# Four seams of a two-layer decoder kernel: where rows are normalised, where one unit is multiplied, in which turn tiles go, and which banks the first units use

## The chip, the cores and the metric

The kernel runs on one NeuronCore of one Trainium2 chip. Its engines are named as in the profile: PE (TensorE) for matmuls, DVE (VectorE), ACT (ScalarE), POOL (GpSimd) and SP (SyncE, which issues the DMAs here). The metric is the device time of one execution in microseconds (us); lower is better.

## The reference, cut to what matters

Two layers over a sequence of 1024 rows of 1024 float32 values. Layer 0 has a gated delta-net mixer with 8 heads, layer 1 a forgetting attention with 16 heads. Both end in the same tail:

```
y = (mixer output) @ w_out                      # 1024x1024 @ 1024x1024
x = layer_norm(DN_ALPHA * x + y, ln_g[i], ln_b[i])
gate = sigmoid(x @ ple_w_gate[i])
x = x + gate * (p[i] @ ple_w_proj[i])
```

`layer_norm` takes mean and variance of each row, then multiplies by `g` and adds `b`.

## The kernel before

Every product of full precision is made of three matmuls (high by high, high by low, low by high), with the operands split by ACT (high part, a copy) and DVE or POOL (low part, a subtraction). Rows go in 8 tiles of 128, columns in halves of 512, the inner dimension in 8 blocks k of 128. So one half of one tile is 8 x 3 = 24 matmuls of 128x512, and a whole tile is 48.

The program is a row of stages, each a `Phase`: an own set of buffers and semaphores, and a barrier over all engines at its end. In order: input transpose; `delta_net` (gdn); `mixer_out` (m0); `gated_embedding` (e0); `fox_values` (fv); `fox_attention` (fa); `mixer_out` again (m1); `gated_embedding` again (e1). Within a stage each engine runs its instructions in the order in which they are written, and waits for semaphores of the others. A helper (`Step`) makes each DVE, ACT and POOL instruction finish before the next begins.

**gdn.** For each head, 64 steps `s` interleave the projection of the next head with the delta rule of the last one. In the last round (`it == H`) no head is left to project, and `part_work` puts parts of m0's product there: a part is one half of one tile over the inner blocks k = 0 to 6 (the heads that are done), 21 matmuls. There are `PARTS = 7` of them, the two halves of tiles 0, 1, 2 and the first half of tile 3. From step 15 on each step takes one k (three matmuls); what isn't done by step 59 (`AT_O_SUMS`) follows in a row at step 60. DVE adds each part to ALPHA times the residual in `take_part`, at the steps in `TAKE_PARTS`, into rows of `x1`. At step 62 (`AT_O_NORM`) DVE finishes the last head in two instructions (lines 915 and 916).

**m0 and m1** (`mixer_out`). `o_part(t)` splits tile t of the mixer's output (ACT `o_hi`, then DVE `o_lo`, line 1130). PE multiplies tile by tile into four PSUM tensors `out[t % 4]`. DVE then, for each tile: two mixes (residual plus product, lines 1158 or 1160) with a `bn_stats` each, `bn_aggr`, a wait for ACT's 1/sqrt (lines 1119 and 1120), the normalising instruction (1168) and the multiplication by the gain (1172). POOL adds the shift and writes the tile to `x1` (line 1182); for the last tile DVE does that itself (1173). DVE's `o_part(t + 2)` stands between `bn_aggr` and the normalising instruction. In m0 the tiles 0 to 2 are short (only k = 7 is left: 6 matmuls each, and one piece of `o_part`), tile 3 is half short, and 4 to 7 are whole. They run in the order 0 to 7. In m1 all tiles are whole; tiles 0 and 1 run together while `w_out` arrives. Both stages begin with nine rounds of small matmuls (`warm_up`).

**e0 and e1** (`gated_embedding`). PE transposes tiles of `x1` (`flip_piece`), ACT and DVE split them into `a_hi`, `a_lo` (two buffers), and PE multiplies them with the gate weights. These come through a ring of 4 half-row blocks that SP fills; block n waits until block n - 4 is split. In e0 the finished tiles are transposed again into `xh`, `xl` for layer 1.

**fa**. `project` makes the units of pair 0 (four units of 24 matmuls: q and k, two halves) before there are any scores. All units go to one PSUM bank, `unit`, and `take_unit` (ACT) copies each out before the next begins. After the four units of a pair come `cross` (POOL), `square` (ACT), `sum_squares` (PE), `root` (ACT) and the multiplication by the gains (DVE, line 2128), and then the first score.

Of the kernel before, what the change touches and what calls it, by code (L numbers as in the profile page):

```python
# [7 lines left out]
F32R = mybir.dt.float32r  # L8
# [241 lines left out]
PARTS = 7  # L250
TAKE_PARTS = (28, 30, 37, 44, 51, 58, 61)
# [736 lines left out]
def mixer_out(nc, c, ring, ahead, after, o, parts, residual, w_out, ln_g, ln_b, w_hi, w_lo, x1, name):  # L988


    with Phase(nc, name) as ph:
# [19 lines left out]
        alone = parts // 2  # L1011

        def pieces(t):

            return [slice(KT - 1, KT)] if t < alone else [slice(0, 4), slice(4, KT)]

        def pieces_before(t):
            return sum(len(pieces(n)) for n in range(t))
# [6 lines left out]
        def _(sp):  # L1025
            def load_x(t):
                if t >= alone + 2:
                    sp.wait_ge(mixed_made, t - 1)
                sp.dma_start(old[:, t % 2], residual[t * P:(t + 1) * P, :]).then_inc(x_loaded[t % 2], 16)
# [6 lines left out]
            load_x(alone)  # L1036
            load_x(alone + 1)
# [5 lines left out]
            for t in range(alone + 2, NT):  # L1043
                load_x(t)

        @block.tensor
        def _(pe):
            def multiply(t, k, halves=(0, 1)):
                if t >= 4:
                    pe.wait_ge(mixed_made, t - 3)  # L1050
                y = out[t % 4]
                for half in halves:
                    if k not in own_ks(t, half):
                        continue
                    first = k == own_ks(t, half)[0]
                    cols = slice(half * HALF, (half + 1) * HALF)
                    pe.matmul(y[:, cols], o_hi[:, t % OB, k, :], w_hi[:, k, cols], start=first, stop=False)  # L1057
                    pe.matmul(y[:, cols], o_hi[:, t % OB, k, :], w_lo[:, k, cols], start=False, stop=False)
                    mm = pe.matmul(y[:, cols], o_lo[:, t % OB, k, :], w_hi[:, k, cols], start=False,
                                   stop=(k == KT - 1))  # L1060
# [13 lines left out]
            for t in range(0 if parts else 2, NT):  # L1074
                pe.wait_ge(o_low, pieces_before(t + 1))
                if t == NT - 1:

                    for half in range(2):
                        for k in range(KT):
                            multiply(t, k, (half,))  # L1080
                    break
                for k in range(KT):
                    multiply(t, k)

        def halves(t):
            for n, ks in enumerate(pieces(t)):
                yield pieces_before(t) + n, ks, o[:, ks, t * P:(t + 1) * P]

        @block.scalar
        def _(act):  # L1090
# [23 lines left out]
            for t in range(NT):  # L1114
# [3 lines left out]
                r = rstd[:, t % 2:t % 2 + 1]  # L1118
                step(act.activation(r, moments[:, t % 2, 1:2], ACT.Ln, bias=eps[:, 0:1]))
# [3 lines left out]
        def _(dve):  # L1123
# [20 lines left out]
            for t in range(NT):  # L1144
                b = t % 2
                if t >= alone:
                    dve.wait_ge(x_loaded[b], 16 * ((t - alone) // 2 + 1))
                if t >= 2:

                    dve.wait_ge(x_made, t - 1)  # L1150
                for half in range(2):
                    cols = slice(half * HALF, (half + 1) * HALF)
                    if half == 0 and t == NT - 1:
                        dve.wait_ge(half_made, 1)
                    else:
                        dve.wait_ge(y_made, t + 1)
                    if 2 * t + half < parts:
                        mix = dve.tensor_tensor(mixed[:, b, cols], x1[:, t, cols], out[t % 4][:, cols], ALU.add)
                    else:
                        mix = dve.scalar_tensor_tensor(mixed[:, b, cols], old[:, b, cols], ALPHA, out[t % 4][:, cols],  # L1160
                                                       ALU.mult, ALU.add)
# [1063 lines left out]
```

## Time and profile before

| | us |
|---|---|
| median of 3 runs | 1812.75 |
| lowest and highest | 1812.61, 1815.48 |
| the profiled execution | 1813.67 |
| its span in the trace | 1811.9 |

The rows of the trace that are used stand in the section after the next. Times in them are microseconds from the start of the span. A timeline row is: start, duration, engine, line, operation, output<-inputs, count, and in brackets how long the engine was idle before it and what ended that. PE's matmuls overlap, so their duration (0.39) is longer than the distance from one to the next.

### The profile page before, as it was taken

Reading aid. Unit: us, or ns where it says so; the run is one execution under the profiler, and the core shown is the slowest. Engines: PE = TensorE matmul, PEld = TensorE weight load, DVE = VectorE, ACT = ScalarE, POOL = GpSimd, SP = SyncE. Lnnn points to the kernel's source line nnn. Section 1 sums busy time; section 2 is a strip of 40 time slices with the busy share of each in tenths; the row PEclk is TensorE's granted clock in tenths of the full one; section 3 lists DMA queues with packets and bytes.
Section 4 is the critical chain, followed back from the end, with each engine's and each line's share of the span. In section 5 each row is a group of like instructions: output and inputs, shape, how many; then the busy total and the mean of one; then the engine's idle time right before and its main releaser. Section 6 shows DMA issues by size and latency. Waiting matters only on the chain. (4 is left out here: it accounts for less than half of the span.)

```text
span 1811.9 us, 29013 instructions
## 1 busy us (share of the span) xinstructions
PE 1711.3 (94%) x11245; PEld 1304.0 (72%) x11245; DVE 909.1 (50%) x1712; ACT 756.8 (42%) x1248; POOL 299.1 (17%) x243
## 2 busy tenths in 40 slices
PE   7999999999999987979989999999999999898898
PEld 5777777777777765868877887666666665687687
DVE  3767576675767724654430300244444544565433
ACT  3446354463645542142231211465556565530411
POOL 2222132221321251200000000222212121012000
PEclk9999999999999998989989999999999999899899
DMA  5121110211101121131130200211111101040311
GB/s 131 48 60 34 26 48 12 48 36 36 42 19 36 59 94 59 35 125 44 41 118 1 70 25 23 56 33 42 48 31 43 42 21 42 15 163 34 117 44 50
DMA packets 113080, 92.86 MB, mean 51 GB/s; under 512 B 19697, under 2 KB 95665, under 8 KB 112945
## 3 DMA queue, kind: packets, MB, share of 16 engines
q1 hardware_dynamic: 112944, 91.02, 17.5%
q8 instruction: 90, 1.47, 0.3%
q14 instruction: 46, 0.37, 0.1%
HBM read 82.51 MB, written 8.49 MB: 50 GB/s over the span
## 5 line engine op out<-in xcount | busy, mean ns | idle before, releaser
L481 PE MATMUL gdn_unit<-part_hi,gdn_w_hi 128*128 128x512 f32 x512 | 232.2, 454 | 0.0
L483 PE MATMUL gdn_unit<-part_hi,gdn_w_lo 128*128 128x512 f32 x512 | 201.7, 394 | 0.0
L482 PE MATMUL gdn_unit<-part_lo,gdn_w_hi 128*128 128x512 f32 x512 | 200.8, 392 | 0.0
L2088 DVE CUSTOM_DVE_ANT_0 fa_probs<-fa_scores,fa_decay 128x896 f32<-128x896 f32 (+7 forms) x128 | 97.0, 757 | 121.6 <-PE fa_scores L1900 74.0
L875 DVE SCALAR_TENSOR_TENSOR x<-gdn_raw,gdn_taps,x 128x512 f32<-128x512 f32 x144 | 119.7, 832 | 5.1
L1852 PE MATMUL fa_unit<-part_hi,fa_w_hi 128*128 128x512 f32 x256 | 115.0, 449 | 4.8 <-ACT fa_qk L1999 3.4
L446 POOL TENSOR_TENSOR gdn_w_lo<-ring,gdn_w_hi 128x1024 fp32r<-128x1024 f32 x31 | 75.4, 2434 | 253.9 <-ACT gdn_w_hi L676 253.9
L483 PEld LDWEIGHTS gdn_unit<-part_hi,gdn_w_lo 128*128 128x128 f32 x512 | 96.2, 188 | 21.6
L2034 ACT ACTIVATE fa_probs_t<-fa_turned 128x512 f32<-128x512 f32 (+1 forms) x96 | 52.3, 544 | 139.3 <-PE fa_turned L1917 138.7
L481 PEld LDWEIGHTS gdn_unit<-part_hi,gdn_w_hi 128*128 128x128 f32 x512 | 97.0, 189 | 16.5 <-issue 3.6
L2028 ACT ACTIVATE fa_probs<-fa_probs,fa_top 128x896 f32<-128x896 f32 (+7 forms) x128 | 99.4, 777 | 22.5 <-DVE fa_top L2088 18.9
L482 PEld LDWEIGHTS gdn_unit<-part_lo,gdn_w_hi 128*128 128x128 f32 x512 | 97.3, 190 | 12.8 <-issue 3.6
L1289 PE MATMUL e_gate<-e_w_hi,e_a_hi 128*128 128x512 f32 x256 | 103.0, 402 | 2.8 <-DVE e_a_lo L1426 2.8
L1854 PE MATMUL fa_unit<-part_hi,fa_w_lo 128*128 128x512 f32 x256 | 100.7, 394 | 0.0
L1917 PE MATMUL fa_turned<-ident,fa_probs 128*128 128x128 f32 x576 | 96.6, 279 | 3.8 <-ACT fa_probs L2028 2.6
L1853 PE MATMUL fa_unit<-part_lo,fa_w_hi 128*128 128x512 f32 x256 | 100.1, 391 | 0.0
L1291 PE MATMUL e_gate<-e_w_hi,e_a_lo 128*128 128x512 f32 x256 | 100.1, 391 | 0.0
L1290 PE MATMUL e_gate<-e_w_lo,e_a_hi 128*128 128x512 f32 x256 | 99.8, 390 | 0.0
L1917 PEld LDWEIGHTS fa_turned<-ident,fa_probs 128*128 128x128 f32 x576 | 68.4, 140 | 41.2 <-issue 15.6
L1057 PE MATMUL m_y<-part_hi,m_o_hi 128*128 128x512 f32 x207 | 82.4, 398 | 7.9 <-DVE m_o_lo L1130 7.9
L2095 DVE COPY fa_probs_t<-fa_turned 128x512 f32<-128x512 f32 (+3 forms) x96 | 47.1, 491 | 75.8 <-PE fa_turned L1917 74.8
L1900 PE MATMUL fa_scores<-fa_qk 64*128 64x512 f32 (+3 forms) x384 | 79.3, 517 | 2.6 <-DVE fa_qk L2128 1.7
(307 smaller groups left out, 3644.4 us busy)
## 6 DMA issues: line engine op xcount, KB each, us to landing
ring<-in_gdn_w_in_dram SPq DMA_DIRECT2D x32, 512.0 KB, 4.1
ring<-in_ple_w_gate_dram SPq DMA_DIRECT2D x32, 256.0 KB, 3.0
ring<-in_fox_w_in_dram SPq DMA_DIRECT2D x32, 256.0 KB, 3.1
ring<-in_fox_w_in_dram SPq DMA_DIRECT2D x16, 512.0 KB, 4.7
fa_decay<-c_rows_scratch SPq DMA_DIRECT2D x64, 128.0 KB, 3.1
in_x_tile<-in_x_dram SPq DMA_DIRECT2D x8, 512.0 KB, 6.3
gdn_g_bc<-g_rows_scratch SPq DMA_DIRECT2D x8, 512.0 KB, 8.5
x_scratch<-x SPq DMA_DIRECT2D x8, 512.0 KB, 2.9
```

The costliest lines, as they stand in the source:

```text
L481: pe.matmul(out, w_hi[:, j % 2, k, :], xh[:, k, ts], start=(k == 0), stop=False)
L482: pe.matmul(out, w_hi[:, j % 2, k, :], xl[:, k, ts], start=False, stop=False)
L483: mm = pe.matmul(out, w_lo[:, j % 2, k, :], xh[:, k, ts], start=False, stop=(k == KT - 1))
L875: step(dve.scalar_tensor_tensor(out, shifted, weight, out, ALU.mult, ALU.add), conv_made if part == TAPS - 1 else None)
L1289: pe.matmul(out[:, cols], hi, w_hi[:, k, cols], start=first, stop=False)
L1290: pe.matmul(out[:, cols], hi, w_lo[:, k, cols], start=False, stop=False)
L1291: mm = pe.matmul(out[:, cols], lo, w_hi[:, k, cols], start=False, stop=end)
L1852: pe.matmul(out, w_hi[:, j % 2, k, :], xh[:, k, ts], start=(k == 0), stop=False)
L1853: pe.matmul(out, w_hi[:, j % 2, k, :], xl[:, k, ts], start=False, stop=False)
L1854: mm = pe.matmul(out, w_lo[:, j % 2, k, :], xh[:, k, ts], start=False, stop=(k == KT - 1))
L1917: mm = pe.transpose(turned[by][:, b * P:(b + 1) * P], probs[:, n % 3, j * P:(j + 1) * P], c["ident"][:])
L2028: step(act.activation(own, own, ACT.Exp, bias=top[:, n % 4:n % 4 + 1], scale=-1.0, accum_out=total[:, p % 2, e, head:head + 1]), exped)
```

## The change

Four things are done.

1. `PARTS` becomes 8: the second half of tile 3 is a part too. It runs at step 60 of the last round, after the seventh, and DVE takes it at step 61.
2. In `mixer_out` with parts (m0) the tiles go in the turns 0, 4, 1, 5, 2, 6, 3, 7, short and whole ones alternating. In both m0 and m1, DVE's `o_part(i + 2)` moves from behind `bn_aggr` to ahead of the mixes. In m0 the warm-up is 4 rounds, not 9.
3. The last tile's mixes go straight to its rows of `x1`, its mean, variance and 1/sqrt to a small tensor `final`, and `mixer_out` ends there. `gated_embedding` loads gain and shift again (two DMAs that write 512 KB each) and normalises the tile in two DVE instructions at t = 4; PE waits for that before it transposes tile 7. To make room, `a_hi`, `a_lo` lie in `part_hi`, `part_lo`.
4. In fa the units 0 to 3 go to the four banks of `scores`; `unit` is used from unit 4 on.

```diff
-PARTS = 7
-TAKE_PARTS = (28, 30, 37, 44, 51, 58, 61)
+PARTS = 8
+TAKE_PARTS = (28, 30, 37, 44, 51, 58, 60, 61)
...
+        turns = (0, 4, 1, 5, 2, 6, 3, 7) if parts else tuple(range(NT))
+        whole = [t for t in turns if 2 * t + 1 >= parts]
...
-            warm_up(pe, c, out[3])
+            warm_up(pe, c, out[3], 4 if parts else 9)
...
-                r = rstd[:, t % 2:t % 2 + 1]
-                step(act.activation(r, moments[:, t % 2, 1:2], ACT.Ln, bias=eps[:, 0:1]))
+                r, var = rstd[:, t % 2:t % 2 + 1], moments[:, t % 2, 1:2]
+                if t == NT - 1:
+                    r, var = final[:, 2:3], final[:, 1:2]
+                step(act.activation(r, var, ACT.Ln, bias=eps[:, 0:1]))
...
-            for t in range(NT):
-                b = t % 2
...
+            for i, t in enumerate(turns):
+                b = i % 2
+                if i and i + 2 < NT:
+                    o_part(i + 2)
...
-                step(dve.bn_aggr(moments[:, b], stats[:, b]), var_made)
-                if t and t + 2 < NT:
-                    o_part(t + 2)
-                dve.wait_ge(rstd_made, t + 1)
+                    row = (x1[:, t] if i == NT - 1 else mixed[:, b])[:, cols]
...
+                step(dve.bn_aggr(final[:, 0:2] if i == NT - 1 else moments[:, b], stats[:, b]), var_made)
+                if i == NT - 1:
+                    break
+                dve.wait_ge(rstd_made, i + 1)
...
-            step(dve.tensor_tensor(x1[:, NT - 1], mixed[:, b], shift[:], ALU.add))
...
             load_p(0)
             load_p(1)
+            sp.dma_start(gain[:], ln_g.partition_broadcast(P)).then_inc(ln_loaded, 16)
+            sp.dma_start(shift[:], ln_b.partition_broadcast(P)).then_inc(ln_loaded, 16)
...
+            def normalise_final():
+                row = x1[:, NT - 1]
+                dve.wait_ge(ln_loaded, 32)
+                step(dve.scalar_tensor_tensor(row, row, final[:, 0:1], gain[:], ALU.subtract, ALU.mult))
+                step(dve.scalar_tensor_tensor(row, row, final[:, 2:3], shift[:], ALU.mult, ALU.add), normal)
...
+                if t == 4:
+                    normalise_final()
                 add(t - 1, 0)
...
+        def unit_bank(it, u):
+
+            return unit[:] if it else scores[u // 2][:, u % 2 * HALF:(u % 2 + 1) * HALF]
...
-                    if n:
+                    if n > 4:
                         pe.wait_ge(unit_taken, n)
```

On DVE, the end of gdn (line 968 is `take_part`, 915 and 916 the last head):

```order
 L968 SCALAR_TENSOR_TENSOR x1<-gdn_raw,gdn_unit1 128x512
 L968 SCALAR_TENSOR_TENSOR x1<-gdn_raw,gdn_unit0 128x512
+L968 SCALAR_TENSOR_TENSOR x1<-gdn_raw,gdn_unit1 128x512
 L915 SCALAR_TENSOR_TENSOR o_t<-o_t,gdn_gain,gdn_eg 128x1024
 L916 TENSOR_TENSOR o_t<-o_t,x1 128x1024
```

The eighth part is taken between the seventh and the two instructions of the last head.

On DVE, the second tile of m0 before, from the first tile's gain on:

```order
L1172 TENSOR_TENSOR m_mixed<-m_mixed,m_gain 128x1024
L1158 TENSOR_TENSOR m_mixed<-x,m_y 128x512
L1163 BN_STATS m_stats<-m_mixed 128x6
L1158 TENSOR_TENSOR m_mixed<-x,m_y 128x512
L1163 BN_STATS m_stats<-m_mixed 128x6
L1164 BN_AGGR m_moments<-m_stats 128x2
L1130 TENSOR_TENSOR m_o_lo<-o_t,m_o_hi 128x512 x2
L1168 TENSOR_SCALAR m_mixed<-m_mixed,m_moments,m_rstd 128x1024
```

and after, from the same gain on (1180 is the gain, 1135 `o_lo`, 1166 and 1168 the mixes):

```order
L1180 TENSOR_TENSOR m_mixed<-m_mixed,m_gain 128x1024
L1135 TENSOR_TENSOR m_o_lo<-o_t,m_o_hi 128x512 x2
L1168 SCALAR_TENSOR_TENSOR m_mixed<-m_old,m_y 128x512
L1171 BN_STATS m_stats<-m_mixed 128x6
L1168 SCALAR_TENSOR_TENSOR m_mixed<-m_old,m_y 128x512
L1171 BN_STATS m_stats<-m_mixed 128x6
L1172 BN_AGGR m_moments<-m_stats 128x2
L1176 TENSOR_SCALAR m_mixed<-m_mixed,m_moments,m_rstd 128x1024
```

The split of a later tile now follows the gain directly, and nothing stands between `bn_aggr` and the normalising instruction.

On SP, the start of e0 after:

```order
L1258 DMA e0_p_tile<-in_p_dram 128x256 x2
L1262 DMA e0_gain<-in_ln_g_dram 128x1024
L1263 DMA e0_shift<-in_ln_b_dram 128x1024
L1255 DMA ring<-in_ple_w_gate_dram 128x512 x16
L60 DMA ring<-in_fox_w_in_dram 128x512 x4
```

Before, the sixteen weight blocks followed the two of `p_tile` directly.

## Rows read from the trace of the kernel before

**Rows 1.** Busy time of m0 by engine: PE, PEld, DVE, ACT, POOL, then clock, DMA share, GB/s.

```profile
706.86:781.71 74.85, 60.08 (x255) 49.53 (x256) 49.15 (x71) 12.52 (x31) 16.70 (x7) 0.89 0.15 50
```

**Rows 2.** Timeline of PE, then DVE, where gdn ends.

```profile
701.67 0.39 PE L534 MATMUL gdn_unit<-part_hi,gdn_w_lo 128*128 128x512 f32 x1
...
702.15 0.69 DVE L968 SCALAR_TENSOR_TENSOR x<-gdn_raw,gdn_unit 128x512 f32<-128x512 f32 x1 [6.36 <-PE gdn_unit L534]
...
704.20 1.23 DVE L916 TENSOR_TENSOR o_t<-o_t,x 128x1024 f32<-128x1024 f32 x1
```

**Rows 3.** Timeline of PE in m0.

```profile
706.88 3.87 PE L122 MATMUL m_y<-tri,ident 128*128 128x128 f32 x18 [4.82 <-PEq L49]
...
722.75 0.79 PE L1057 MATMUL m_y<-part_hi,m_o_hi 128*128 128x512 f32 x1 [7.87 <-DVE m_o_lo L1130]
723.34 0.63 PE L1058 MATMUL m_y<-part_lo,m_o_hi 128*128 128x512 f32 x1
...
727.18 0.47 PE L1058 MATMUL m_y<-part_lo,m_o_hi 128*128 128x512 f32 x1
```

**Rows 4.** Timeline of DVE in m0.

```profile
712.25 0.69 DVE L1158 TENSOR_TENSOR m_mixed<-x,m_y 128x512 f32<-128x512 f32 x1 [4.00 <-PE m_y L1059]
...
716.03 0.81 DVE L1168 TENSOR_SCALAR m_mixed<-m_mixed,m_moments,m_rstd 128x1024 f32<-128x1024 f32 x1 [0.67 <-ACT m_rstd L1120]
...
718.14 0.69 DVE L1158 TENSOR_TENSOR m_mixed<-x,m_y 128x512 f32<-128x512 f32 x1
...
721.28 1.42 DVE L1130 TENSOR_TENSOR m_o_lo<-o_t,m_o_hi 128x512 fp32r<-128x512 f32 x2
...
753.20 0.69 DVE L1160 SCALAR_TENSOR_TENSOR m_mixed<-m_old,m_y 128x512 f32<-128x512 f32 x1 [4.21 <-PE m_y L1059]
...
764.08 0.69 DVE L1160 SCALAR_TENSOR_TENSOR m_mixed<-m_old,m_y 128x512 f32<-128x512 f32 x1 [4.21 <-PE m_y L1059]
...
779.42 1.22 DVE L1173 TENSOR_TENSOR x<-m_mixed,m_shift 128x1024 f32<-128x1024 f32 x1
```

**Rows 5.** Timelines where m0 and m1 end: ACT; ACT, DVE, ACT.

```profile
781.71 1.29 ACT L1387 ACTIVATE e_w_hi<-ring 128x512 fp32r<-128x512 f32 x2 [4.49 <-PEq L49]
...
1672.54 0.20 ACT L1120 ACTIVATE m_rstd<-m_rstd 128x1 f32<-128x1 f32 x1
...
1674.96 1.23 DVE L1173 TENSOR_TENSOR x<-m_mixed,m_shift 128x1024 f32<-128x1024 f32 x1
...
1677.68 1.29 ACT L1387 ACTIVATE e_w_hi<-ring 128x512 fp32r<-128x512 f32 x2 [4.93 <-PEq L49]
```

**Rows 6.** Timelines of DVE and POOL early in gdn; last, POOL in m0.

```profile
61.26 1.54 DVE L875 SCALAR_TENSOR_TENSOR x<-gdn_raw,gdn_taps,x 128x512 f32<-128x512 f32 x2
...
63.35 4.34 DVE L875 SCALAR_TENSOR_TENSOR x<-gdn_raw,gdn_taps,x 128x512 f32<-128x512 f32 x3
...
63.53 2.83 POOL L446 TENSOR_TENSOR gdn_w_lo<-ring,gdn_w_hi 128x1024 fp32r<-128x1024 f32 x1 [8.79 <-ACT gdn_w_hi L676]
...
718.25 2.35 POOL L1182 TENSOR_TENSOR x<-m_mixed,m_shift 128x1024 f32<-128x1024 f32 x1 [21.66 <-DVE m_mixed L1172]
```

**Rows 7.** Timelines at fa's start: PE, ACT, POOL.

```profile
1120.39 0.47 PE L1852 MATMUL fa_unit<-part_hi,fa_w_hi 128*128 128x512 f32 x1 [1.47 <-DVE fa_w_lo L2115]
...
1126.94 0.47 PE L1852 MATMUL fa_unit<-part_hi,fa_w_hi 128*128 128x512 f32 x1 [0.86 <-ACT fa_qk L1999]
...
1149.39 1.11 ACT L2021 ACTIVATE fa_probs_t<-fa_scores,fa_eps 128x1024 f32<-128x1024 f32 x1 [0.31 <-PE fa_scores L1884]
...
1143.69 4.38 POOL L1821 TENSOR_TENSOR fa_probs_t<-fa_qk 64x512 f32<-64x512 f32 x4
```

**Rows 8.** E0's start on ACT; DMA in m0 (KB, us to landing); DVE in e0.

```profile
793.99 0.38 ACT L1361 ACTIVATE e_p_hi<-e_flip 128x256 fp32r<-128x256 f32 x1 [4.02 <-PE e_flip L1278]
...
m_shift<-in_ln_b_dram SPq DMA_DIRECT2D x1, 512.0 KB, 6.3
...
857.67 0.69 DVE L1439 SCALAR_TENSOR_TENSOR e_tanh<-e_tanh,e_proj 128x512 f32<-128x512 f32 x1 [2.41 <-PE e_proj L1291]
```

More of the change, by code:

```diff
@@ L1010, in mixer_out, with pieces, pieces_before @@
         block = ph.enter_context(nc.Block())
[L1011 to L1018, printed above, removed]
+        turns = (0, 4, 1, 5, 2, 6, 3, 7) if parts else tuple(range(NT))
+        whole = [t for t in turns if 2 * t + 1 >= parts]
+        def pieces(i):
+            return [slice(KT - 1, KT)] if turns[i] not in whole else [slice(0, 4), slice(4, KT)]
+        def pieces_before(i):
+            return sum(len(pieces(n)) for n in range(i))
         def own_ks(t, half):
@@ L1042, in _, with multiply @@
                 after.start(sp)
-            for t in range(alone + 2, NT):
-                load_x(t)
+            for n in range(2, len(whole)):
+                load_x(n)
         @block.tensor
         def _(pe):
[L1048 to L1051, printed above, removed]
+            def multiply(i, k, halves=(0, 1)):
+                if i >= 4:
+                    pe.wait_ge(mixed_made, i - 3)
+                y = out[i % 4]
                 for half in halves:
-                    if k not in own_ks(t, half):
+                    if k not in own_ks(turns[i], half):
                         continue
-                    first = k == own_ks(t, half)[0]
+                    first = k == own_ks(turns[i], half)[0]
                     cols = slice(half * HALF, (half + 1) * HALF)
-                    pe.matmul(y[:, cols], o_hi[:, t % OB, k, :], w_hi[:, k, cols], start=first, stop=False)
-                    pe.matmul(y[:, cols], o_hi[:, t % OB, k, :], w_lo[:, k, cols], start=False, stop=False)
-                    mm = pe.matmul(y[:, cols], o_lo[:, t % OB, k, :], w_hi[:, k, cols], start=False,
+                    pe.matmul(y[:, cols], o_hi[:, i % OB, k, :], w_hi[:, k, cols], start=first, stop=False)
+                    pe.matmul(y[:, cols], o_hi[:, i % OB, k, :], w_lo[:, k, cols], start=False, stop=False)
+                    mm = pe.matmul(y[:, cols], o_lo[:, i % OB, k, :], w_hi[:, k, cols], start=False,
                                    stop=(k == KT - 1))
@@ L1159, in _ @@
                     else:
-                        mix = dve.scalar_tensor_tensor(mixed[:, b, cols], old[:, b, cols], ALPHA, out[t % 4][:, cols],
-                                                       ALU.mult, ALU.add)
+                        mix = dve.scalar_tensor_tensor(row, old[:, whole.index(t) % 2, cols], ALPHA,
+                                                       out[i % 4][:, cols], ALU.mult, ALU.add)
                     step(mix, mixed_made if half else None)
-                    step(dve.bn_stats(stats[:, b, half], mixed[:, b, cols]))
@@ L1178, in _, with gated_embedding @@
             pool.wait_ge(ln_loaded, 32)
-            for t in range(NT - 1):
-                pool.wait_ge(scaled, t + 1)
-                step(pool.tensor_tensor(x1[:, t], mixed[:, t % 2], shift[:], ALU.add), x_made)
-def gated_embedding(nc, c, ring, ahead, after, x1, p_emb, w_gate, w_proj, out_dram, xh, xl, stored, name):
+            for i in range(NT - 1):
+                pool.wait_ge(scaled, i + 1)
+                step(pool.tensor_tensor(x1[:, turns[i]], mixed[:, i % 2], shift[:], ALU.add), x_made)
+def gated_embedding(nc, c, ring, ahead, after, x1, p_emb, w_gate, w_proj, out_dram, xh, xl, stored, final, ln_g, ln_b, spare, name):
     KP = p_emb.shape[1] // P
@@ L1274, in flip_piece @@
                     pe.wait_ge(half_used, 2 * piece[1] + 2)
+                if piece[0] == "x1" and piece[1] == NT - 1:
+                    pe.wait_ge(normal, 1)
                 if piece[0] == "p":
@@ L1998, in take_unit @@
                 act.wait_ge(unit_made, n + 1)
-                step(act.activation(qk[:, it % 2, u // 2, u % 2 * HALF:(u % 2 + 1) * HALF], unit[:], ACT.Copy),
+                step(act.activation(qk[:, it % 2, u // 2, u % 2 * HALF:(u % 2 + 1) * HALF], unit_bank(it, u), ACT.Copy),
                      unit_taken)
```

69 lines of the change are left out of this document (38 added, 31 removed).

## The prediction

> **What bounds the kernel now.** I read the busy time by stretch first, to see which stages PE fills and which not, and then the timelines of the engines around the four seams. PE is the bound of the kernel; between stages it stands still, and in m0 it works 60.08 of 74.85 us [rows 1]. There are four places to look at.
>
> Where gdn ends, PE's last matmul starts at 701.67; DVE takes the part at 702.15, finishes the last head until 704.20 + 1.23 = 705.43, and only then the barrier opens and m0 begins, at 706.88 [rows 2, 3]. In m0's first half DVE is the bound: a short tile costs PE 6 matmuls but DVE 5.89 us (712.25 to 718.14, with 0.67 of waiting for ACT's 1/sqrt) [rows 4]. Since the split of tile 3 stands in DVE's order behind the second tile (721.28, two pieces in 1.42), PE waits 7.87 us for it, and its next matmuls take 0.63 instead of the 0.39 of the others [rows 2 to 4]: TensorE's clock is at the lower level, 1.2 GHz, and the granted clock of the whole stage is 0.89 [rows 1]. From then on PE is the bound: whole tiles follow each other in 764.08 - 753.20 = 10.88 us, 0.227 per matmul, and DVE waits 4.21 for each [rows 4]. Where m0 and m1 end, DVE finishes the last tile alone: 779.42 + 1.22 = 780.64, and e0 begins at 781.71, 1.07 later; in m1 the same at 1676.19 and 1677.68, 1.49 later [rows 4, 5]. At fa's start one unit follows the other only when its bank has been copied out: 1126.94 - 1120.39 = 6.55 us for 24 matmuls that take 5.44, so 1.11 of waiting at each [rows 7].
>
> **The eighth part.** 21 matmuls go from m0 to the end of gdn. They follow the seventh part at step 60 without a wait: 21 x 0.227 = 4.76 us of PE. Nothing covers them. DVE's take of the eighth part stands ahead of the last head's two instructions and waits for PE, as its take of the seventh now waits 6.36 [rows 2]. The seventh is taken (0.69) while PE works; then the eighth, then the two instructions as now (702.84 to 705.43). So gdn ends **4.76 later**. This is not work beside the last head, it is in front of it.
>
> **m0.** I count from its start, 0 (now 706.86 on ACT). Warm-up: 18 matmuls in 3.87 become 8 in 1.7. That 0.21 per matmul held for nearly all of the 18, so the clock rose near 3.4; matmuls after the 7.87 gap, with no warm-up at all, needed 727.18 - 722.75 = 4.4 [rows 3]. I take 3.4, so that the first 4 matmuls of 512 columns run at (727.18 - 723.34) / 9 = 0.427 and 50 at 0.227. Tile 0 and the whole tile 4 are ready for DVE at 15.0; a rise at 5 instead costs 0.7.
>
> From there DVE is the bound. A tile costs it 5.89, now always with the wait for 1/sqrt, since the split that used to cover it has moved. The split of a later tile adds 1.45 for a whole one and 0.34 for a short one (one piece of 128 columns per row).
>
> To this comes a price that the order of DVE's instructions hides. Look at gdn [rows 6]: two instructions of line 875 take 1.54, three take 4.34 where POOL starts its subtraction 0.18 after the first of them. Alone they would take 2.33. POOL waited for the first of the three to end (so its 2.83), and the second stood still until POOL was done. In m0 POOL's shift begins 0.14 after the gain's end (718.25 against 718.11) [rows 4, 6]. Until now a mix followed there, with one operand in PSUM, and it kept its 0.69 beside POOL (718.14) [rows 4]. After the change the split follows, which like line 875 reads two SBUF operands: its first piece begins 0.03 after the gain, POOL waits for it, and its second piece waits for POOL. By the row that is 4.34 - 2.33 = **2.0 us** for every whole tile whose split follows a gain. A short tile has one piece and pays nothing. I take this value, since the row shows the very order of events; the ends are 0 and, if the single pieces paid too, 2.0 for each.
>
> The Trainium skill, SBUF — State Buffer, section "Who interferes with whom", says so as a rule: a DVE instruction with two SBUF inputs and a GpSimd instruction that reads SBUF exclude each other, and whoever is first holds the shared ports for the whole instruction. By that rule, the trace agrees (2.0 us lost in rows 6), and the rule speaks against putting the split where the change puts it: m0 would take 61.7 with it and 57.7 without.
>
> The chain on DVE, then: second turn 15.0 to 20.9 (its split, 3.45 long, lies in the wait before 15.0); third 0.34 + 5.89 to 27.1; fourth 1.45 + 2.0 + 5.89 to 36.5; fifth 0.34 + 5.89 to 42.7; sixth 1.45 + 2.0 + 5.89 to 52.0; seventh 5.89 to 57.9; the last only its mixes, statistics (3.1) and ACT's two steps (0.6) to **61.7**. PE gets the sixth turn's operand at 30.6 and the last one's at 46.1, so it waits 2.2 and 3.3 us and ends near 57.1, or 59 if the clock falls in the second wait; DVE needs the last half at 59.4, so this too stays hidden. Now the stage takes 780.64 - 706.86 = 73.8. So m0 gives back **12.1**, of which 3.45 is the last tile's normalisation.
>
> **m1.** Its last tile ends with ACT at 1672.54 + 0.20 instead of DVE at 1676.19 [rows 5]: **3.45** less; the barrier is taken as it is. Here too each split is ahead of the mixes and pays 2.0, so a tile costs DVE 1.45 + 2.0 + 5.89 = 9.3. That is under PE's 10.88, and what the first tiles fall behind is caught up by the sixth.
>
> **fa.** Three waits of 1.11 go. ACT copies unit 3 3.4 earlier; its squares follow, and then `root`, now at 1149.39 [rows 7]. POOL's four products (4.38, from 1143.69) hang on the third copy and move only 2.2 forward, to 1145.8; `root` of the first kind needs two of them, and the second kind's is wanted at 1148.2. So the first score comes **3.4** earlier. POOL's split of the next weights ends right before its products, so then near 1141.4; unit 4 wants it at 1120.4 + 4 x 5.44 = 1142.2, 0.8 later.
>
> **e0 and e1.** Two broadcasts now stand on SP's queue ahead of sixteen weight blocks, which wait for 0.9 of issue and for 1 MB of traffic. In m0 the same two, behind 1 MB of `m_old`, took 6.3 to land [rows 8]. As an estimate from that row they hold up the first weight blocks by 2.5 to 3.5. ACT has split these by 793.99 - 4.02 = 789.97 and then idles 4.02 until PE gives it work [rows 8], so they may come that late: nothing. The two normalising instructions (1.2 to 1.3 each, as the 1.22 of line 1173 over the same 1024 columns [rows 4]) fall in a DVE wait of 2.41 in e0 [rows 8] and a longer one in e1: 0.2 at most.
>
> **The sum.** 4.8 - 12.1 - 3.45 - 3.4 = -14.2 on the profiled execution's 1813.67, giving 1799.5. That execution is 0.9 above the median of 1812.75, so the median after is **1798.5**. The ends: 0 instead of 2 x 2.0 at the splits gives 1794.5. Single pieces that pay (+4), and a late rise of the clock (+0.7), give 1803.2.
>
> **The rivals.**
> - POOL and DVE do not exclude each other here (other tensors, other kinds of operand than line 875's). Then m0 takes 57.7 and the time is 1794.5. For it: no row shows the split itself beside POOL. Against: rows 6.
> - The weight blocks do come late, in both e stages. If the delay goes through in full, at 2.5 for each stage, it is +5: 1803.5. Against: the 4.02 of idle ACT right there.
> - The change doesn't do in fa what it says: `root` waits for another than the copies, as POOL's products. Then 2.2 instead of 3.4 is gained, or nothing: 1799.7 to 1802.
> - Slower: the clock. The shorter warm-up and the new waits of 2.2 and 3.3 leave PE at 1.2 GHz through m0. Its 216 matmuls at 0.427 last 92 us instead of 49 and become the bound: 31 more than my 61.7, 1829. It decides from some 115 matmuls at the lower level, where m0's PE needs more than 61.7 + 14.2. Against: after 7.87 of waiting and without warm-up the clock was back after 4.4 us of matmuls.
>
> **Chances.** My forecast 0.70, with its own spread of about 2 us; no exclusion 0.12; late blocks 0.08; fa 0.06; slower 0.03; a mixture 0.01. The range is 1793.5 to 1803.5. A measurement of this kernel can tell about 0.2% (3.6 us) from no change: under 1809.1 is faster, 0.96; 0.01 the same; 0.03 slower.
>
> **What would show it.** The profile after should have: gdn's last matmul 4.8 later; a split of about 3.4 (two pieces) behind every gain of m0 that a whole tile's split follows; PE waiting for `o_lo` before the sixth and the last turn, DVE without waits for `y` from the second turn on; e0 beginning near 774.4, fa's first score 14.2 - 3.45 = 10.8 earlier, e1 14.2 earlier. I am wrong if the split keeps its 1.42 beside POOL, if ACT in e0 waits for the first weight blocks, or if m0's matmuls stay at 0.63.

## The result, and the profile after

The changed kernel takes 1819.97 us (median of 7 runs, 1818.14 to 1821.39) where the kernel before took 1813.89 in the same comparison: a ratio of 1.003, with a 95% interval of 1.002 to 1.0041. It is 6 us slower, 0.3%, and the interval lies clear of 1. The forecast was 1798.5, a gain of 14.

The first view to read is the page's busy time by engine. Before:

```profile
PE 1711.3 (94%) x11245; PEld 1304.0 (72%) x11245; DVE 909.1 (50%) x1712; ACT 756.8 (42%) x1248; POOL 299.1 (17%) x243
```

After:

```profile
PE 1728.6 (95%) x11235; PEld 1302.5 (72%) x11235; DVE 924.2 (51%) x1710; ACT 756.7 (42%) x1247; POOL 302.5 (17%) x243
```

PE is 17.3 us busier, although the change moves wide matmuls (those of 512 columns) and adds none; it drops ten 128-column warm-ups. No step of the forecast has such a term. The seams, on the other hand, look much as forecast. Timeline of DVE of the kernel after, at gdn's end and in m0:

```profile
711.41 0.69 DVE L968 SCALAR_TENSOR_TENSOR x<-gdn_raw,gdn_unit 128x512 f32<-128x512 f32 x1 [4.22 <-PE gdn_unit L534]
...
713.45 1.22 DVE L916 TENSOR_TENSOR o_t<-o_t,x 128x1024 f32<-128x1024 f32 x1
...
726.79 3.50 DVE L1135 TENSOR_TENSOR m_o_lo<-o_t,m_o_hi 128x512 fp32r<-128x512 f32 x2
732.45 0.69 DVE L1168 SCALAR_TENSOR_TENSOR m_mixed<-m_old,m_y 128x512 f32<-128x512 f32 x1 [2.16 <-PE m_y L1061]
...
744.67 3.46 DVE L1135 TENSOR_TENSOR m_o_lo<-o_t,m_o_hi 128x512 fp32r<-128x512 f32 x2
```

The eighth part costs DVE a wait of 4.22 before its take. Each split of a whole tile behind a gain takes 3.46 to 3.50, where [rows 4] had 1.42: so the price of 2.0 for POOL is there, and POOL pays its share in the same place:

```profile
726.90 2.84 POOL L1189 TENSOR_TENSOR x<-m_mixed,m_shift 128x1024 f32<-128x1024 f32 x1 [26.02 <-DVE m_mixed L1180]
738.51 2.44 POOL L1189 TENSOR_TENSOR x<-m_mixed,m_shift 128x1024 f32<-128x1024 f32 x1 [8.77 <-DVE m_mixed L1180]
```

(POOL's timeline of the kernel after; the first shift has a whole tile's split beside it, the second only a short one's.) m0 by engine, from the view of stretches, to be held against [rows 1] (PE, PEld, DVE, ACT, POOL, clock, DMA share, GB/s):

```profile
716.12:780.62 64.50, 56.04 (x224) 44.43 (x225) 51.00 (x67) 11.56 (x29) 18.10 (x7) 0.92 0.14 50
```

ACT's timeline of the kernel after where m0 ends, early in e0, and where m1 ends, against [rows 5, 8]:

```profile
779.33 0.20 ACT L1125 ACTIVATE final<-final 128x1 f32<-128x1 f32 x1
780.62 1.30 ACT L1400 ACTIVATE e_w_hi<-ring 128x512 fp32r<-128x512 f32 x2 [1.09 <-PEq L49]
...
789.73 1.29 ACT L1400 ACTIVATE e_w_hi<-ring 128x512 fp32r<-128x512 f32 x2 [2.16 <-DMA ring<-in_ple_w_gate_dram]
793.83 0.38 ACT L1374 ACTIVATE e_p_hi<-e_flip 128x256 fp32r<-128x256 f32 x1 [2.81 <-PE e_flip L1291]
...
1679.92 0.20 ACT L1125 ACTIVATE final<-final 128x1 f32<-128x1 f32 x1
1681.54 1.30 ACT L1400 ACTIVATE e_w_hi<-ring 128x512 fp32r<-128x512 f32 x2 [1.42 <-PEq L49]
```

e0 now begins 1.09 behind ACT's last step, where it began 1.07 behind DVE's before. In e0 ACT waits 2.16 for the weight blocks that the two broadcasts hold up. The prediction had named such a wait as a sign that it is wrong; but ACT then still waits 2.81 for PE, so the blocks' lateness is hidden, as the forecast had it. And in fa the four units follow each other without a wait; PE's timeline has the first at 1126.61 and the first score at 1158.47, 31.86 later, where it came 34.90 later before.

PE's timeline of m0 shows what the two waits for `o_lo` did to the clock:

```profile
748.19 0.50 PE L1059 MATMUL m_y<-part_hi,m_o_hi 128*128 128x512 f32 x1 [1.88 <-DVE m_o_lo L1135]
748.52 0.44 PE L1060 MATMUL m_y<-part_lo,m_o_hi 128*128 128x512 f32 x1
748.76 0.63 PE L1061 MATMUL m_y<-part_hi,m_o_lo 128*128 128x512 f32 x1
...
752.17 0.40 PE L1060 MATMUL m_y<-part_lo,m_o_hi 128*128 128x512 f32 x1
```

Just after the first wait the matmuls take 0.63, the duration of the lower level, for 3.4 us; then they are back at 0.40, and after the second wait (1.33, at 763.92) they stay there. DVE is last in m0, so this costs the stage nothing.

So where are the 20 us that the forecast missed? The wide matmuls are slower in every stage, also in stages that the change doesn't touch. fv is one, and there PE works almost without a pause. Groups of instructions by line (count, busy us, mean ns of one), before:

```profile
L482 PE MATMUL gdn_unit<-part_lo,gdn_w_hi 128*128 128x512 f32 x512 | 200.8, 392 | 0.0
...
L1291 PE MATMUL e_gate<-e_w_hi,e_a_lo 128*128 128x512 f32 x256 | 100.1, 391 | 0.0
...
L1544 PE MATMUL fv_bank<-part_hi,fv_w_lo 128*128 128x512 f32 x128 | 49.8, 389 | 0.0
```

After:

```profile
L482 PE MATMUL gdn_unit<-part_lo,gdn_w_hi 128*128 128x512 f32 x512 | 202.4, 395 | 0.0
...
L1304 PE MATMUL e_gate<-e_w_hi,part_lo 128*128 128x512 f32 x256 | 101.1, 395 | 0.0
...
L1565 PE MATMUL fv_bank<-part_hi,fv_w_lo 128*128 128x512 f32 x128 | 50.6, 396 | 0.0
```

The same matmuls in the timeline of PE, in the middle of fv, before:

```profile
1050.20 0.39 PE L1542 MATMUL fv_bank<-part_hi,fv_w_hi 128*128 128x512 f32 x1
...
1051.56 0.39 PE L1542 MATMUL fv_bank<-part_hi,fv_w_hi 128*128 128x512 f32 x1
```

After:

```profile
1049.62 0.40 PE L1563 MATMUL fv_bank<-part_hi,fv_w_hi 128*128 128x512 f32 x1
...
1051.02 0.40 PE L1563 MATMUL fv_bank<-part_hi,fv_w_hi 128*128 128x512 f32 x1
```

Six matmuls take 1.36 us before and 1.40 after: 0.227 and 0.233 for each. Where PE has nothing else to do, the mean distance from one matmul's start to the next is 0.2267 before and 0.2333 after. The clock is no reason: over the whole run it is 0.978 before and 0.980 after. Groups of other shapes are unchanged (1280 matmuls of 64x32 at 223 ns in both).

### The profile page after: what moved, and what is told of

The parts are those of the page before. It is cut to its first block and busy times, and to the rows that moved or that the text cites. A ratio compares the mean times of both kernels' runs of the same rounds, so it can differ in the third digit from the quotient of the medians.

```text
span 1818.2 us, 28998 instructions
## 1 busy us (share of the span) xinstructions
PE 1728.6 (95%) x11235; PEld 1302.5 (72%) x11235; DVE 924.2 (51%) x1710; ACT 756.7 (42%) x1247; POOL 302.5 (17%) x243
## 5 line engine op out<-in xcount | busy, mean ns | idle before, releaser
L1302 PE MATMUL e_gate<-e_w_hi,part_hi 128*128 128x512 f32 x256 | 104.4, 408 | 3.1 <-DVE part_lo L1439 2.7
L1877 PE MATMUL fa_unit<-part_hi,fa_w_hi 128*128 128x512 f32 x224 | 102.8, 459 | 0.0
L1303 PE MATMUL e_gate<-e_w_lo,part_hi 128*128 128x512 f32 x256 | 101.1, 395 | 0.0
L1304 PE MATMUL e_gate<-e_w_hi,part_lo 128*128 128x512 f32 x256 | 101.1, 395 | 0.0
L1878 PE MATMUL fa_unit<-part_lo,fa_w_hi 128*128 128x512 f32 x224 | 88.5, 395 | 0.0
L1879 PE MATMUL fa_unit<-part_hi,fa_w_lo 128*128 128x512 f32 x224 | 88.3, 394 | 0.0
```

The costliest lines, as they stand in the source:

```text
L1302: pe.matmul(out[:, cols], hi, w_hi[:, k, cols], start=first, stop=False)
L1303: pe.matmul(out[:, cols], hi, w_lo[:, k, cols], start=False, stop=False)
L1304: mm = pe.matmul(out[:, cols], lo, w_hi[:, k, cols], start=False, stop=end)
L1877: pe.matmul(out, w_hi[:, j % 2, k, :], xh[:, k, ts], start=(k == 0), stop=False)
L1878: pe.matmul(out, w_hi[:, j % 2, k, :], xl[:, k, ts], start=False, stop=False)
```

## What the experiments ask

The one edit that touches everything is the smallest: `final = sb("final", [P, 3])`, 12 bytes per partition, allocated behind `ring` and ahead of all tensors of the stages. (It is not among the lines of the diff shown with the change.) The built program lists where tensors start: `gdn_w_hi` at 160896 before and at 160928 after; `part_hi`, `part_lo`, `x1` and `ring`, allocated earlier, stay. All later tensors have moved by 32 bytes. My theory became that this slows the wide matmuls; the rival is that the change's instructions do. All times below are medians, with the ratio to the kernel before of the same comparison.

### Is it the addresses?

```diff
-        final = sb("final", [P, 3])
+        final = sb("final", [P, 32])      # after_pad128; 16 in after_pad64
```

> The kernel after, with `final` 32 numbers wide instead of 3 (the surplus is unused), so that every tensor allocated behind it starts 128 bytes further than in the kernel before, where the kernel after has them 32 bytes further (start addresses as the built program lists them: gdn_w_hi at 160896 before, 160928 after, 161024 here). Theory, addresses: nearly all matmuls of 512 columns in two F32R operands take 3 to 7 ns longer after (389 -> 396 ns for m_y, e_gate and fv_bank, 392 -> 395 in gdn), PE's busy time 17 us more (1728.6 against 1711.3) in code the change doesn't touch, because one operand of each starts 32 bytes off a wider boundary. Then here the means return to 389 to 392 and the time is 1820 - 17 = 1803, between 1799 and 1806. Rival, the change's instructions themselves (other order, other program length, other load on PE) slow the matmuls: the means stay at 395 and the time at 1820.

> The kernel after, with `final` 16 numbers wide: everything behind it starts 64 bytes further than before (gdn_w_hi at 160960). Addresses matter by 64 bytes: as the 128-byte version, 1799 to 1806. They matter by 128: matmuls slow, 1815 to 1825. Rival, not the addresses: 1820.

```diff
         ring = sb("ring", [P, 2, D])
+        gap = sb("gap", [P, 8])           # before_shift32; 64 in before_shift256
```

> The kernel before with an unused tensor of 8 numbers per partition at the place where the change puts `final`: not one instruction differs, only the addresses of what is allocated behind it, 32 bytes further. Theory, addresses: the matmuls of 512 columns take 395 instead of 389 to 392, PE's busy time is 1728 instead of 1711 and the time 1814 + 17 = 1831, between 1825 and 1834. Rival, the change's instructions: 1814 as before.

Measured: before_shift32 takes 1827.65 (ratio 1.0075, 1.0059 to 1.009), 13 us more than the kernel before, with the same instructions. That much settles that addresses matter. Groups by line of before_shift32:

```profile
L1291 PE MATMUL e_gate<-e_w_hi,e_a_lo 128*128 128x512 f32 x256 | 100.2, 391 | 0.0
...
L1544 PE MATMUL fv_bank<-part_hi,fv_w_lo 128*128 128x512 f32 x128 | 50.6, 396 | 0.0
```

fv has gone to 396, but the e stages are still at 391, which my expectation (17 us, all stages) had missed, hence 13 and not 17. And after_pad64 takes 1815.88 (1.0009, 0.9999 to 1.0018), after_pad128 1816.23 (1.001, 1.0 to 1.002): 4 us better than after, not 17. Both expectations failed: moving everything by 64 or by 128 bytes doesn't restore the matmuls. In most stages their means are 392 to 396, for example in after_pad128:

```profile
L1565 PE MATMUL fv_bank<-part_hi,fv_w_lo 128*128 128x512 f32 x128 | 50.5, 395 | 0.0
```

So "start on a wider boundary" is not the rule. What distinguishes the e stages of before_shift32? There both operands of a matmul, `e_a_*` and `e_w_*`, lie behind the gap and have moved together. In fv one operand is `part_hi` or `part_lo`, which stays, and the other moves. In the kernel after, the e stages are slow too (395 above), and there the tiles lie in `part_hi`, which has not moved. That gives a second theory: the distance between the two operands.

### Distance or place?

after_first allocates `final` ahead of `part_hi`; after_pad512 makes it 128 wide.

```diff
+        final = sb("final", [P, 3])       # after_first
         part_hi, part_lo = sb("part_hi", [P, KT, T], F32R), sb("part_lo", [P, KT, T], F32R)
         x1 = sb("x1", [P, NT, D])
         ring = sb("ring", [P, 2, D])
-        final = sb("final", [P, 3])
```

> The kernel after with `final` (3 numbers per partition) allocated ahead of part_hi instead of behind `ring`. All operands of the wide matmuls then move by the same 32 bytes, so their absolute addresses are as odd as in the kernel after (gdn_w_hi at 160928, as after) but the distance between any two of them is that of the kernel before (part_hi 18080 to gdn_w_hi 160928 = 142848, before 18048 to 160896 = 142848). Theory, distance: in the runs so far a stretch was at 389 ns and 0.227 per matmul wherever the two operands' distance was a multiple of 512 bytes, as in the whole kernel before and in e0 and e1 of the one with 32 bytes of gap, and at 392 to 398 ns and 0.229 to 0.2335 elsewhere. Then it is 389 everywhere here and the time falls to what I forecast for the change, 1798.5, between 1794 and 1804. Rival, absolute address: 395 ns, 1816 to 1822.

> The kernel after with `final` 128 numbers wide: all behind it 512 bytes further than in the kernel before, so distances stay multiples of 512. Theory, distance modulo 512: 389 ns everywhere, 1794 to 1804, equal to the kernel with `final` first within 2 us. Rival, only the exact places of before are fast (or a modulus above 512): 392 or more, 1810 to 1820.

> The kernel before with an unused tensor of 64 numbers (256 bytes) at the same place. It asks for the modulus: if distances count modulo 256, 389 ns and 1814; if modulo 512, 391 to 396 ns in gdn, m0, fv and fa, 389 in e0 and e1, and 1818 to 1828.

Measured: after_first 1801.14 (0.9928, 0.9913 to 0.9943), after_pad512 1800.65 (0.9927, 0.9911 to 0.9944), before_shift256 1813.14 (0.9996, 0.9986 to 1.0007). Groups by line of after_first, whose `gdn_w_hi` lies at 160928 as in the kernel after:

```profile
L482 PE MATMUL gdn_unit<-part_lo,gdn_w_hi 128*128 128x512 f32 x512 | 200.6, 392 | 0.0
...
L1304 PE MATMUL e_gate<-e_w_hi,part_lo 128*128 128x512 f32 x256 | 100.0, 391 | 0.0
...
L1565 PE MATMUL fv_bank<-part_hi,fv_w_lo 128*128 128x512 f32 x128 | 49.8, 389 | 0.0
```

The distance theory holds: the weights lie at the same absolute places as in the kernel after, and the speed is that of before. The distance of before, 142848 bytes from `part_hi` to `gdn_w_hi`, is a multiple of 256 bytes; shifts of 0, 256 and 512 from it are fast (so my guess of 512 was too strict), and shifts of 32, 64 and 128 are slower, by up to 0.0066 us for each matmul. Other shifts were not tried. fv alone separates the two kinds without overlap: it lasts 195.7 to 197.2 us in the ten traces of kernels at the fast distances, and 200.3 to 201.7 in the five at the others. The whole price in the changed kernel is 1819.97 - 1801.14 = **18.8 us**.

### The two operands of one matmul, or another pair?

```diff
 def fox_values(...):
+        gap = sb("gap", [P, 8])
         w_hi, w_lo = sb("w_hi", [P, 2, KT, HALF], F32R), sb("w_lo", [P, 2, KT, HALF], F32R)
```

> The kernel before with an unused tensor of 32 bytes inside fox_values alone, ahead of its w_hi, so that only fv's weight buffers (and the small tensors behind them) move against part_hi and part_lo; gdn, m0, the e stages, fa and m1 keep every address. Theory, the distance between the two operands of a matmul: only fv's 768 wide matmuls go from 389 to 396 ns and 0.2267 to 0.2333 each, the rest of the program stays, and fv takes 768 x 0.0066 = 5 us longer: 1814 + 5 = 1819. Rival, some other pair (operands against what other engines read and write, or one tensor's absolute place): no change in fv, 1814, or a change outside fv.

Measured: 1818.2 (1.0021, 1.0012 to 1.0031), 3.8 more than before. Groups by line of gap_in_fv:

```profile
L482 PE MATMUL gdn_unit<-part_lo,gdn_w_hi 128*128 128x512 f32 x512 | 200.6, 392 | 0.0
...
L1291 PE MATMUL e_gate<-e_w_hi,e_a_lo 128*128 128x512 f32 x256 | 100.1, 391 | 0.0
...
L1545 PE MATMUL fv_bank<-part_hi,fv_w_lo 128*128 128x512 f32 x128 | 50.6, 396 | 0.0
```

Only fv is slow. From its start to fa's first wide matmul it takes 201.67 instead of 196.89, 4.8 of the 5.1 that 768 x 0.0066 gives. It could still be that PE's operands collide with what another engine reads or writes. One stretch of fv settles that, since in it all others are idle. Stretches of before and of gap_in_fv (busy time and records of PE, PEld, DVE, ACT and POOL, then clock, DMA share, GB/s):

```profile
945.00:960.00 15.00, 15.00 (x68) 12.43 (x67) 0.00 (x0) 0.00 (x0) 0.00 (x0) 1.00 0.00 1
945.00:960.00 15.00, 15.00 (x66) 12.06 (x65) 0.00 (x0) 0.00 (x0) 0.00 (x0) 1.00 0.00 1
```

DVE, ACT, POOL and the DMA share are at 0, the clock is 1.00 in both, and gap_in_fv still gets two matmuls fewer into the same 15 us. So what collides is read by PE itself. In the timelines each weight load (PEld) starts together with the matmul ahead of it (in before, the matmul of line 1542 and the load of line 1543 both at 1050.20): while a matmul streams its moving operand, the stationary one of the next is read. That these two reads get in each other's way at some distances is my reading; the runs show that it is the distance between the two tensors that counts, and that no other engine is needed for it.

The Trainium skill (TensorE: Matmul & The Clock Gate, Part 2: What happens when you issue a matmul) says that loading the next weights takes no read bandwidth from the running matmul, since PE has two independent read ports. By that rule the distance between the two could not matter. Here it costs 0.2333 - 0.2267 = 0.0066 a matmul, 3%, when it is 32 bytes off a multiple of 256, with nothing but PE at work. If my reading of the pair is right, the measurement decides against the rule as an unconditional one.

### The change without its addresses

From here on after_first is the base. Five kernels take one part back or move it. Their medians come from 4 runs each and different comparisons; stages of the same code differ by 1 to 2 us from one execution to the next, so differences of that size are read from the traces, between the same two instructions.

**POOL beside the splits.** split_early:

```diff
-                if t and t + 2 < NT:      # ACT, ahead of the wait for var_made
-                    o_part(t + 2)
+                if t + 3 < NT:
+                    o_part(t + 3)
...
-                if i and i + 2 < NT:      # DVE, ahead of the turn's mixes
-                    o_part(i + 2)
...
                 step(dve.bn_aggr(...), var_made)
+                if i + 3 < NT:
+                    o_part(i + 3)
                 dve.wait_ge(rstd_made, i + 1)
```

> Measured against after_first (1801.1), with its addresses. In mixer_out ACT and DVE split tile i + 3 behind turn i's bn_aggr, instead of tile i + 2 at the start of turn i, that is behind the previous gain. Theory, POOL and DVE exclude each other: after the gain POOL's shift (2.8) and the split's second piece stand in each other's way (3.45 to 3.50 for two pieces in after_first, three times); behind bn_aggr POOL has nothing to do, two pieces take 1.42, and they also cover the wait of 0.7 for ACT's 1/sqrt. By hand from after_first's rows: second turn 16.2 from m0's start (its y is PE's), then 5.9, 6.6, 5.9, 6.6, 5.9, 5.9 and 3.1 + 0.5 for the last: m0 takes 57 instead of 63.3, 1795, between 1793.5 and 1797. m1 gains nothing, PE is its bound. Rival: the 3.5 has another cause (the tile's own kind of instruction, two F32R pieces): the pieces keep 3.5 here, m0 takes 62 to 63, 1800 to 1801.

Measured: 1792.99 (0.9886, 0.987 to 0.9903), 8.1 below the base. Timeline of DVE in m0:

```profile
719.91 1.42 DVE L1135 TENSOR_TENSOR m_o_lo<-o_t,m_o_hi 128x512 fp32r<-128x512 f32 x2
721.37 0.81 DVE L1176 TENSOR_SCALAR m_mixed<-m_mixed,m_moments,m_rstd 128x1024 f32<-128x1024 f32 x1
...
737.22 1.42 DVE L1135 TENSOR_TENSOR m_o_lo<-o_t,m_o_hi 128x512 fp32r<-128x512 f32 x2
```

The very same instruction takes 1.42 where POOL is idle and 3.45 to 3.50 beside POOL's shift, and the wait for 1/sqrt behind it is gone. m0 runs from 712.05 to ACT's last step at 769.06, 57.0, as worked out, 6.3 less than the base's 63.3. The time fell by more, to 0.5 below the expected range; the rest is not explained.

**The eighth part.** seven_parts:

```diff
-PARTS = 8
-TAKE_PARTS = (28, 30, 37, 44, 51, 58, 60, 61)
+PARTS = 7
+TAKE_PARTS = (28, 30, 37, 44, 51, 58, 61)
```

> after_first with seven parts instead of eight, taken at the steps of the kernel before. Theory: the eighth part's 21 matmuls are exposed in gdn (gdn ends 4.76 earlier here, m0's start near 706.9 instead of 711.4), but in m0 the sixth tile's second half costs PE the same 4.76 and a second split beside POOL on DVE, and from the seventh turn PE is again as late as DVE: m0 is 4.6 to 5.5 longer, the total 1801 to 1802, that is the eighth part itself is worth 0 to 1. Rival, the eighth part is what m0's gain comes from (or it only costs): 1805 or 1797.

Measured: 1797.7 (0.9905, 0.9887 to 0.9922), 3.4 below the base, though the intervals still touch (the base's begins at 0.9913). The traces tell it better. In gdn's last round, the last matmuls that wait for POOL are in the base and in seven_parts:

```profile
696.44 1.99 PE L541 MATMUL gdn_w<-gdn_eg,ones 128*128 128x512 f32 x4 [0.27 <-POOL gdn_eg L460]
698.53 1.98 PE L541 MATMUL gdn_w<-gdn_eg,ones 128*128 128x512 f32 x4 [0.27 <-POOL gdn_eg L460]
```

From there to m0's start it is 15.01 in the base (711.45) and 10.25 in seven_parts (708.78): the eighth part costs gdn 4.76, and this execution of seven_parts had merely come there 2.1 later. m0 is 2.2 longer, not 5: its DVE chain from the first whole tile on grew by 3.2, as worked out (0.34 to 1.45 for the split, 2.05 for POOL), but PE was nowhere last, and the first whole tile came 1.1 sooner because the clock rose earlier in this execution (3.8 after m0's start, in the base 5.7). So the eighth part costs 4.76 and gives back 2.2, or 3.2 without that difference in the clock: a net loss of 1.6 to 2.6. My expectation, a gain of 0 to 1, had overrated PE in m0.

**fa's units.** one_bank puts them back into one bank:

```diff
-            return unit[:] if it else scores[u // 2][:, u % 2 * HALF:(u % 2 + 1) * HALF]
+            return unit[:]
...
-                    if n > 4:
+                    if n:
```

> after_first with fa's first four units in the one bank of the kernel before. Theory: three waits of 1.11 for ACT's copy return, and all of it is on the path: the first score comes 3.4 to 3.6 later, 1804.7. Rival, the products of POOL or the weights' split end last: 0 to 2.2 later, 1801 to 1803.3.

Measured: 1803.94 (0.9942, 0.9927 to 0.9957), 2.8 above the base; in the two traces the first score comes 34.92 after fa's first matmul instead of 31.27, that is 3.65. So the whole of the three waits is on the path to the first score; the whole stage fa is 2.5 longer. PE's timeline of one_bank has the wait back:

```profile
1120.42 0.47 PE L1877 MATMUL fa_unit<-part_hi,fa_w_hi 128*128 128x512 f32 x1 [0.87 <-ACT fa_qk L2024]
```

**The last tile.** norm_in_m normalises it at the end of its own stage, in three instructions:

```diff
                 if i == NT - 1:
+                    dve.wait_ge(rstd_made, NT)
+                    step(dve.tensor_scalar(x1[:, NT - 1], x1[:, NT - 1], final[:, 0:1], final[:, 2:3], ALU.subtract, ALU.mult))
+                    step(dve.tensor_tensor(x1[:, NT - 1], x1[:, NT - 1], gain[:], ALU.mult))
+                    step(dve.tensor_tensor(x1[:, NT - 1], x1[:, NT - 1], shift[:], ALU.add))
                     break
...
-                    normalise_final()
+                    dve.wait_ge(ln_loaded, 32)
```

(PE's wait for `normal` goes too.)

> after_first with the last tile of m0 and m1 normalised at the end of its own stage again, by three instructions of DVE as in the kernel before, and nothing in its place in e0 and e1. Theory: 3.4 at the end of m0 and of m1, nothing back from the two freed instructions: 1801.1 + 6.9 = 1808, between 1807 and 1808.5. Rival, the two instructions in e0 and e1 cost there what they save (DVE late for PE): 1802 to 1805.

Measured: 1806.6 (0.9956, 0.9941 to 0.9971), 5.5 above the base and just under the expected range. ACT's timeline of norm_in_m:

```profile
773.43 0.20 ACT L1125 ACTIVATE final<-final 128x1 f32<-128x1 f32 x1
778.24 1.29 ACT L1402 ACTIVATE e_w_hi<-ring 128x512 fp32r<-128x512 f32 x2 [4.61 <-PEq L49]
```

Between them lie 4.61 instead of the base's 1.09, and at m1's end 4.93 instead of 1.42: 3.52 and 3.51. e1 lasts 134.03 in both, so the two instructions cost e1 nothing. The traces say 7.0 for the two ends, the times 5.5; in this execution gdn, which is the same code, ended about 1 earlier than the base's.

**The warm-up.** warm_nine:

```diff
-            warm_up(pe, c, out[3], 4 if parts else 9)
+            warm_up(pe, c, out[3], 9)
```

> after_first with 18 instead of 8 warm-up matmuls at m0's start. In after_first the clock is low until 5.7 after m0's start (forecast 3.4), the first whole tile is ready at 16.2 instead of 15.0. Theory, the short warm-up delays the clock: with 18 it is high near 3.6, the ten more cost 2 us of PE but save the slow matmuls; the first whole tile at 15.5 to 17, the total 1800 to 1801.5, no difference beyond 1. Rival, the clock rises only when the wide matmuls have run as long as now: everything 2 later, 1803.

Measured: 1799.84 (0.9921, 0.9906 to 0.9936), no difference beyond what varies between executions. Its PE timeline at m0's start, which began at 711.06:

```profile
715.90 0.63 PE L1061 MATMUL m_y<-part_hi,m_o_lo 128*128 128x512 f32 x1
716.32 0.44 PE L1059 MATMUL m_y<-part_hi,m_o_hi 128*128 128x512 f32 x1
716.60 0.39 PE L1060 MATMUL m_y<-part_lo,m_o_hi 128*128 128x512 f32 x1
```

The clock is at the higher level from 716.4, 5.3 after the start; in the base, with 8 warm-ups, from 717.1, 5.7 after it. That is 0.4 between the two. But with the same 8 warm-ups the rise comes 3.8 after the start in seven_parts and 6.1 in early_seven, and with 18 it comes 3.8 after it in the kernel before. So the executions differ by more than the two lengths do, and the theory that the short warm-up delays the clock is not borne out.

**A version that beats both.** early_seven is split_early with seven parts.

> split_early (1793.0) with seven parts. In seven_parts the eighth part turned out to cost 2.4 to 3.4 in all: 4.6 exposed in gdn against 2.2 saved in m0, 3.2 of it DVE's split of one more whole tile, with 2.05 for POOL beside it. Behind bn_aggr that split costs only 0.4 of DVE's chain, but PE's 21 matmuls are back in m0 (4.76), and there PE is then last: by hand the last y comes 56.8 after m0's start, m0 takes 59 instead of 57. Theory: 2 longer in m0, 4.57 shorter in gdn: 1790.5, between 1789 and 1792. Rival, PE's lateness in m0 takes it all (4.6): 1793.

Measured: 1791.22 (0.9872, 0.9856 to 0.9889), 23 below the kernel before and 29 below the changed one. It and split_early (1792.99) overlap within their intervals. m0 takes 60.1 (706.86 to 767.00), as DVE now waits for PE at the last tile's second half; DVE's timeline:

```profile
764.73 0.69 DVE L1166 SCALAR_TENSOR_TENSOR x<-m_old,m_y 128x512 f32<-128x512 f32 x1 [2.06 <-PE m_y L1061]
```

So with the splits out of POOL's way the eighth part is worth 3.1 in m0 and costs 4.76 in gdn (15.01 and 10.25 between the same two instructions as above).

## Why the prediction was wrong, step by step

What each stage lasts in the three traces that matter (us; the first row is m0's start, with gdn and what precedes it; the last row is the span; a stage ends where the next begins):

| stage | before | after | after_first | first - before | forecast | after - first |
|---|---|---|---|---|---|---|
| to m0 | 706.88 | 716.14 | 711.45 | +4.6 | +4.8 | 4.7 |
| m0 | 74.83 | 64.48 | 64.34 | -10.5 | -12.1 | 0.1 |
| e0 | 141.79 | 144.70 | 142.37 | +0.6 | 0 | 2.3 |
| fv | 196.89 | 201.29 | 196.17 | -0.7 | 0 | 5.1 |
| fa | 457.86 | 456.78 | 454.59 | -3.3 | -3.4 | 2.2 |
| m1 | 99.43 | 98.15 | 95.45 | -4.0 | -3.45 | 2.7 |
| e1 | 134.2 | 136.7 | 134.0 | -0.2 | 0 | 2.7 |
| sum | 1811.9 | 1818.2 | 1798.4 | -13.5 | -14.2 | 19.8 |

- **The step that failed** is one that the prediction did not have. It priced every instruction that the change adds or moves, and took all others to keep their durations: "0.227 per matmul" was carried from [rows 4] through every sum, and e0, fv and e1 were put at 0. What the runs showed in its place: 0.2333 per matmul in fv and m1, because the tensor `final` shifts one operand of the matmuls by 32 bytes against the other. The change calls `final` a small tensor, and no term asks where it lies. It costs 18.8 us by the times, 19.8 by the spans, and turns a gain of 13 into a loss of 6. m0 alone hardly suffers, as DVE is its bound.
- **The eighth part, +4.76**: right: +4.6 by the stage's start, 4.76 between the same two instructions. It also is, as seven_parts shows, the one part of the change that doesn't pay.
- **m0, -12.1**: the mechanism was right, the size 1.6 too large. The first whole tile came 16.2 after the start instead of 15.0, since the clock rose at 5.7 where I took 3.4 from the warm-up of [rows 3] (in that trace the first wide matmul, 3.6 after the start, still took 0.48); from there the chain took 47.05 where I had 46.7. The forecast had taken the clock's rise as a fixed time, and it varies (3.8 to 6.1 after the start with 8 warm-ups). PE's waits were 2.25 and 1.56 in after_first, where 2.2 and 3.3 were forecast: the first is right, and the second is shorter because the clock fell behind the first wait, for 3.4 us, and not behind the second.
- **The exclusion of POOL and DVE, 2.0 for each whole tile**: right: 3.45 to 3.50 against 1.42. What the forecast did not draw is the consequence: the place behind `bn_aggr` one turn earlier was free, and is worth 6.3 in m0's trace and 8 by the medians.
- **m1, -3.45**: right: norm_in_m, which takes it back, lengthens the stage by 3.5; against the kernel before the stage shows -4.0.
- **fa, -3.4**: right: -3.3 for the stage. one_bank, which takes it back, gives 3.65 at the first score, 2.5 for the stage and 2.8 by the medians.
- **e0 and e1, 0**: right for what the forecast priced there (+0.6 and -0.2 with the addresses of before, no more than executions differ). The late blocks are hidden (2.16 of waiting for DMA ahead of 2.81 of waiting for PE).
- **The rivals**: none came true. The slower one put its loss on PE too, but by the clock in m0. The clock fell in m0 for 3.4 us only, hidden behind DVE, and the loss came from the other stages, of which the forecast had put e0, fv and e1 at 0.

Of the 14.2 forecast, 13.1 are there when the addresses are as before (1801.14 against 1814.25).

## What to carry to other kernels

An allocation is part of a change even when it holds three numbers: list where the operands of the hot matmuls start, before and after, and compare the distances between them. Put small tensors where nothing hot lies behind them, or ahead of both operands. When a time misses the forecast, look first at the mean duration of instructions that nobody touched; a shift of 2% in them is easily taken for noise, and over some 4800 wide matmuls it was the whole result. And of a known collision (POOL's shift against a split with two SBUF operands), ask not only what it costs but which place in the order is free of it.

## What was new about the hardware

- With 512 columns and both operands F32R, a matmul in a dense stretch takes 0.2267 us when its moving and its stationary operand start a multiple of 256 bytes apart (shifts of 0, 256 and 512 bytes), and 0.2333 when they are 32 bytes off. At 64 and 128 bytes off, it takes 0.229 to 0.2335, depending on the stage; what decides between these was not sought.
- The slower rate holds in a stretch where DVE, ACT, POOL and the DMA share are at 0 (66 records of PE in 15 us, against 68).
- The records give the weight load the same duration in both kernels (187 to 190 ns in fv), so its own row doesn't tell; the matmul's does (389 and 396 ns).
- DVE's split with two SBUF operands took 1.42 for two pieces alone and 3.45 to 3.50 with POOL's addition begun beside it, and POOL took 2.79 to 2.84 instead of 2.35 to 2.45.
- In m0 the clock rose 3.8 us (before) and 5.3 us (warm_nine) after the start with 18 warm-up matmuls, and 3.8 (seven_parts) to 6.1 us (early_seven) after it with 8.
- After a wait of 1.88 in m0 of the kernel after, the matmuls were at the lower level for 3.4 us; after one of 1.33 they were not.
